# Two row blocks at the end of a stage: block one normed by column halves and turned as two products with the old residual, and the next unit's low part kept over its raw weights

## What is computed

```
def second_block(x, ...):                       # 256 x 1024
    for i in range(2):
        h = rmsnorm(x, mix_pre_gain[i])
        m = fox_mixer(h, ...) if i == 0 else s5_mixer(h, ...)     # each ends in ... @ w_out
        x = x + rmsnorm(m, mix_post_gain[i])                      # pm0, pm1 of the kernel
        h = rmsnorm(x, ffn_pre_gain[i])
        x = x + rmsnorm((silu(h @ w_gate) * (h @ w_up)) @ w_down, ffn_post_gain[i])   # pf0, pf1
    return x

def rmsnorm(x, gain):
    return x * rsqrt(mean(x * x, -1) + 1e-6) * gain
```

## Time and profile before

| | |
|---|---|
| median of three runs | 1037.14 us (1037.1 to 1037.45) |
| the profiled execution, as timed | 1034.07 us |
| its span in the profile | 1032.4 us |
| share of the span in which PE is busy | 96% |
| VectorE, ScalarE, GpSimd busy | 62%, 47%, 31% |
| granted TensorE clock, mean | 0.989 of full |

### The profile page before, as it was taken

How to read it: one execution, slowest core, us unless ns; L and a number is a source line. 1 busy time by engine, 2 the same in 40 slices (tenths; PEclk the granted TensorE clock), 3 DMA queues, 4 the chain that set the end, 5 groups by cost and what they waited for, 6 DMA issues and landing times.

```text
span 1032.4 us, 16878 instructions
## 1 busy us (share of the span) xinstructions
PE 992.5 (96%) x6874; PEld 880.7 (85%) x6874; DVE 635.4 (62%) x653; ACT 482.0 (47%) x632; POOL 324.2 (31%) x316
## 2 busy tenths in 40 slices
PE   8996999999999899999899999999989999999997
PEld 6984779999988778788689999987958989999885
DVE  4899766677654455466675555545676665555534
ACT  5762564444443456545464444434434464444332
POOL 5692047898899211179410000000100010000000
PEclk9997999999999999999999999999999999999999
DMA  9741036777676845544355655556970645555541
GB/s 337 249 163 41 1 123 196 224 221 219 226 236 215 258 125 181 164 138 156 97 182 172 194 172 194 175 192 223 396 298 4 201 142 186 176 190 177 190 163 41
DMA packets 130081, 186.77 MB, mean 181 GB/s; under 512 B 4720, under 2 KB 103536, under 8 KB 129392
## 3 DMA queue, kind: packets, MB, share of 16 engines
q1 hardware_dynamic: 106032, 158.54, 47.0%
q10 hardware_dynamic: 24000, 27.54, 7.9%
HBM read 174.54 MB, written 15.73 MB: 184 GB/s over the span
## 4 chain that ended last, share of the span: by engine, by line
PE 79%; DVE 11%; ACT 4%; issue 3%; DMA 2%; POOL 0%; ACTq 0%; DVEq 0%; POOLq 0%
PE ps L394 13%; PE ps L396 13%; PE ps L395 13%; PE ps L443 7%; PE ps L447 7%; PE ps L445 7%; PE ps L415 3%; PE ps L417 3%; PE ps L416 3%; DVE cacc L1895 3%; DVE wlo L354 2%; ACT whi L348 2%; DMA wraw<-in_s_w_glu 2%; PE ps L821 1%; PE ps L840 1%
## 5 line engine op out<-in xcount | busy, mean ns | idle before, releaser
L354 DVE TENSOR_TENSOR wlo<-wraw,whi 128x2048 fp32r<-128x2048 f32 x143 | 344.6, 2410 | 238.4 <-ACT whi L348 238.4
L348 ACT ACTIVATE whi<-wraw 128x2048 fp32r<-128x2048 f32 x143 | 273.8, 1915 | 378.3 <-PE ps L396 219.6
L394 PE MATMUL ps<-actH,whi 128*128 128x256 f32 x1232 | 351.7, 285 | 1.3 <-DVE actL L565 1.1
L396 PE MATMUL ps<-actH,wlo 128*128 128x256 f32 x1232 | 348.9, 283 | 0.0
L395 PE MATMUL ps<-actL,whi 128*128 128x256 f32 x1232 | 348.8, 283 | 0.0
L394 PEld LDWEIGHTS ps<-actH,whi 128*128 128x128 f32 x1232 | 236.5, 192 | 4.5 <-issue 3.9
L395 PEld LDWEIGHTS ps<-actL,whi 128*128 128x128 f32 x1232 | 236.6, 192 | 0.1
L396 PEld LDWEIGHTS ps<-actH,wlo 128*128 128x128 f32 x1232 | 236.5, 192 | 0.0
L594 POOL TENSOR_SCALAR rs<-ss 128x1 f32<-128x1 f32 (+2 forms) x16 | 4.1, 253 | 603.7 <-ACT nat L580 490.9
L443 PE MATMUL ps<-whi,gH 128*128 128x512 f32 x264 | 82.0, 392 | 0.0
L447 PE MATMUL ps<-whi,gL 128*128 128x512 f32 x264 | 81.4, 390 | 0.0
(11 more groups left out here) (346 smaller groups left out, 1361.4 us busy)
## 6 DMA issues: line engine op xcount, KB each, us to landing
wraw<-in_ffn_w_gate SPq DMA_DIRECT2D x22, 1024.0 KB, 5.3
wraw<-in_ffn_w_up SPq DMA_DIRECT2D x22, 1024.0 KB, 5.3
wraw<-in_ffn_w_down SPq DMA_DIRECT2D x22, 1024.0 KB, 4.9
wraw<-in_fox_w_in SPq DMA_DIRECT2D x16, 1024.0 KB, 5.5
wraw<-in_w_gate SPq DMA_DIRECT2D x11, 1024.0 KB, 5.4
wraw<-in_w_up SPq DMA_DIRECT2D x11, 1024.0 KB, 5.6
wraw<-in_w_down SPq DMA_DIRECT2D x11, 1024.0 KB, 4.9
wraw<-in_w_in SPq DMA_DIRECT2D x9, 1024.0 KB, 11.4
```

Of the source, the lines that this page charges most:

```text
L348: act.activation(self.whi[:, n0 % RING, :], self.wraw[:, n0 % RAW, :], ACT.Copy).then_inc(self.hi_done, 1)
L354: dve.tensor_tensor(self.wlo[:, n0 % RING, :], self.wraw[:, n0 % RAW, :], self.whi[:, n0 % RING, :].bitcast(F32), ALU.subtract).then_inc(s ...
L394: pe.matmul(out, wh, self.actH[:, k, :], start=(i == 0), stop=False)
L396: last = pe.matmul(out, wl, self.actH[:, k, :], start=False, stop=(i == KT - 1))
```

## The change

Nothing of the result's definition changes. The diff's parts:

- **Squares and norms by halves.** At all four seams the accumulator of each row block is squared, and multiplied by the gain, as two halves of 512 columns. ACT and DVE take different halves at a time, and the square goes to `sg` or `prod`. `mm_k_pair` orders block 1 by column half in the last unit and signals `second` when the first half is done. POOL adds the two sums (one more instruction for each block).
- **Block 1 as two products.** PE no longer waits for the new residual of block 1. DVE makes a diagonal matrix of block 1's root, and PE gets each turned tile of block 1 as (old `x_res` tile) times identity plus (`nat` tile) times that diagonal, summed in PSUM, where before there was one transpose. DVE adds block 1 to the residual after its turn (`dve_post_add`). At pf1, where nothing is turned, the addition stays.
- **The first unit of f2, s and f3** (`apart`) is split early: high part to a third buffer `whi3`, low part over its own raw weights. So its raw buffer is free only when PE has used the unit, and the load four places on waits for that (`unit_used`). In the loops over f2 and f3 the same test holds for every second pair, so the gate load of each such pair waits for `unit_used` too.
- **The unit behind it** is split by ACT after its turn and by DVE after its turn and the late addition.
- **The store** of block 1 is in two column halves, the second issued from ACT. The tables `RTab` and `OTab` are loaded once the fourth square of pf0 is done.

```
+        self.wrawlow = at("wrawlow", [P, RAW, UNIT], F32R, self.where["wraw"])
+        self.whi3 = at("whi3", [P, UNIT], F32R, self.where["Uall"])
+        self.apart = (self.first["f2.up"], self.first["s"], self.first["f3.up"])
...
+    def high_of(self, n):
+        return self.whi3[:] if n in self.apart else self.whi[:, n % RING, :]
+
+    def low_of(self, n):
+
+        return self.wrawlow[:, n % RAW, :] if n in self.apart else self.wlo[:, n % RING, :]
+
     def load_unit(self, sp, n0, view, it=0):
 
         n = n0 + 4 * it
         if n0 >= RAW:
-            sp.wait_ge(self.lo_done, n - RAW + 1)
+            sp.wait_ge(self.used if n0 - RAW in self.apart else self.lo_done, n - RAW + 1)
...
-        if n0 >= RING:
+        if n0 >= RING and n0 not in self.apart:
             act.wait_ge(self.used, n - RING + 1)
-        act.activation(self.whi[:, n0 % RING, :], self.wraw[:, n0 % RAW, :], ACT.Copy).then_inc(self.hi_done, 1)
+        act.activation(self.high_of(n0), self.wraw[:, n0 % RAW, :], ACT.Copy).then_inc(self.hi_done, 1)
 
     def split_low(self, dve, n0, it=0):
 
         n = n0 + 4 * it
         dve.wait_ge(self.hi_done, n + 1)
-        dve.tensor_tensor(self.wlo[:, n0 % RING, :], self.wraw[:, n0 % RAW, :],
-                          self.whi[:, n0 % RING, :].bitcast(F32), ALU.subtract).then_inc(self.lo_done, 1)
+        dve.tensor_tensor(self.low_of(n0), self.wraw[:, n0 % RAW, :],
+                          self.high_of(n0).bitcast(F32), ALU.subtract).then_inc(self.lo_done, 1)
...
+        if second is not None:
+            order = order[0:2]
...
+        if second is not None:
+            for c in range(2):
+                out = self.ps[:, base + 2 + c, :]
+                for k in range(2):
+                    h, l = xh[:, k0 + k, P:2 * P], xl[:, k0 + k, P:2 * P]
+                    hi, lo = (t[:, s, k * 1024 + c * 512:k * 1024 + (c + 1) * 512] for t in (self.whi, self.wlo))
+                    pe.matmul(out, h, hi, start=(k0 + k == 0), stop=False)
+                    pe.matmul(out, h, lo, start=False, stop=False)
+                    last = pe.matmul(out, l, hi, start=False, stop=(k0 + k == kn - 1))
+                if c == 0:
+                    last.then_inc(self.sem(second), 1)
...
+            out, cols = self.tp_spot(kt, banks)[:, r * P:(r + 1) * P], slice(kt * P, (kt + 1) * P)
+            if post and r == 1:
+                pe.matmul(out, self.x[:, 1, cols], self.ident[:], start=True, stop=False)
+                last = pe.matmul(out, self.nat[:, 1, cols], self.rdiag[:, 1, :], start=False, stop=True)
+            else:
+                last = pe.transpose(out, self.x[:, r, cols], self.ident[:])
...
+        if post:
+            pe.wait_ge(*self.past(post + "_normed", 4))
+            pe.wait_ge(*self.past(post + "_turn_diag", 1))
+        else:
+            pe.wait_ge(*self.past(ready, 3))
...
+        for i in range(2 * RT):
+            r = i // 2
+            if st[:2] == "pf" and i == 0:
+                act.wait_ge(*self.past(st + "_scale", 1))
+            act.wait_ge(*(self.past(first, 1), self.past(st + "_normed", 1), self.past(first[:2] + "_second", 1),
+                          (self.used, used))[i])
+            if i > 1:
+                act.wait_ge(*self.past(st + "_squares", i - 1))
+            act.activation((self.sg, self.prod)[i % 2][:], self.ps[:, base + i, :], ACT.Square,
+                           scale=self.rx[:, 8 + r:9 + r] if st[:2] == "pf" else D ** -0.5,
+                           accum_out=self.ss[:, i:i + 1]).then_inc(self.sem(st + "_squares"), 1)
...
+    def pool_post_rstd(self, pool, st):
+
+        if st[:2] == "pf":
+            pool.tensor_scalar(self.rx[:, 8:8 + RT], self.rx[:, 0:RT], D ** -0.5, None, ALU.mult)\
+                .then_inc(self.sem(st + "_scale"), 1)
+        for r in range(RT):
+            half, rs = self.ss[:, 8 + r:9 + r], self.rs[:, r:r + 1]
+            pool.wait_ge(*self.past(st + "_squares", 2 * r + 1))
+            pool.tensor_scalar(half, self.ss[:, 2 * r:2 * r + 1], EPS, None, ALU.add)\
+                .then_inc(self.sem(st + "_first_var"), 1)
+            pool.wait_ge(*self.past(st + "_first_var", r + 1))
+            pool.wait_ge(*self.past(st + "_squares", 2 * r + 2))
+            pool.tensor_tensor(rs, self.ss[:, 2 * r + 1:2 * r + 2], half, ALU.add)\
+                .then_inc(self.sem(st + "_var"), 1)
+            pool.wait_ge(*self.past(st + "_var", r + 1))
+            pool.tensor_tensor(rs, rs, self.mhalf[:, 0:1], ALU.pow).then_inc(self.sem(st + "_rstd"), 1)
...
+    def dve_postnorm(self, dve, st, base, gain, gain_ready, gain_value, first):
+
+        def norm(i):
+            h = slice(512 * (i % 2), 512 * (i % 2) + 512)
+            t, acc, g = self.nat[:, i // 2, h], self.ps[:, base + i, :], gain[:, h]
+            if st[:2] == "pf":
+                j = dve.scalar_tensor_tensor(t, acc, self.rx[:, i // 2:i // 2 + 1], g, ALU.mult, ALU.mult)
+            else:
+                j = dve.tensor_tensor(t, acc, g, ALU.mult)
+            j.then_inc(self.sem(st + "_normed"), 1)
 
         dve.wait_ge(*self.past(gain_ready, gain_value))
+        dve.wait_ge(*self.past(first, 1))
+        norm(1)
+        dve.wait_ge(*self.past(st + "_squares", 1))
+        norm(0)
+        dve.wait_ge(*self.past(st + "_squares", 3))
+        norm(2)
+        dve.wait_ge(*self.past(st + "_normed", 2))
+        dve.wait_ge(*self.past(st + "_rstd", 1))
+        self.dve_post_add(dve, st, 0)
+        dve.wait_ge(*self.past(st + "_squares", 4))
+        norm(3)
+        dve.wait_ge(*self.past(st + "_rstd", 2))
+        if st == "pf1":
+            dve.wait_ge(*self.past(st + "_normed", 4))
+            self.dve_post_add(dve, st, 1)
+        else:
+            dve.tensor_scalar(self.rdiag[:, 1, :], self.ident[:], self.rs[:, 1:2], None, ALU.mult)\
+               .then_inc(self.sem(st + "_turn_diag"), 1)
+
+    def dve_post_add(self, dve, st, r):
+
+        for c in range(2):
+            h = slice(512 * c, 512 * c + 512)
+            dve.scalar_tensor_tensor(self.x[:, r, h], self.nat[:, r, h], self.rs[:, r:r + 1], self.x[:, r, h],
+                                     ALU.mult, ALU.add).then_inc(self.sem(st + "_x_ready"), 1)
...
+                for i in range(3):
+                    pair(n + 2 * i, 256 * i, None)
+                with sp.Fori(1, (FP - 1) // 2) as it:
...
-            for r in range(RT):
-                sp.wait_ge(*m.past("pf1_x_ready", 2 * r + 2))
-                sp.dma_start(out[0, r * P:(r + 1) * P, :], m.x[:, r, :]).then_inc(sem("stored"), 16)
-            sp.wait_ge(*m.past("stored", 16 * RT))
+            sp.wait_ge(*m.past("pf1_x_ready", 2))
+            sp.dma_start(out[0, 0:P, :], m.x[:, 0, :]).then_inc(sem("stored"), 16)
+            sp.wait_ge(*m.past("pf1_x_ready", 3))
+            sp.dma_start(out[0, P:2 * P, 0:512], m.x[:, 1, 0:512]).then_inc(sem("stored"), 16)
+            sp.wait_ge(*m.past("stored", 16 * 2))
+            sp.wait_ge(*m.past("last_stored", 16))
...
             m.act_post_squares(act, "pm0", 4, "o2_first", n + 4)
-            m.split_high(act, n + 5)
-            act.wait_ge(*m.past("pm0_normed", RT))
+            act.wait_ge(*m.past("pm0_normed", 2 * RT))
             act.dma_start(m.gb[0][:], io["mix_post_gain_2"][1:2, :].to_broadcast([P, D])).then_inc(sem("gain0_in"), 16)
             m.act_turn(act, "f2", (0, 1, 2, 3, 6, 7), gain=FFNPRE)
+            m.split_high(act, n + 5)
             m.act_pre_squares(act, "f2", "pm0_x_ready")
             m.act_ffn(act, "f2", 4)
 
             n = first["s"]
             m.act_post_squares(act, "pf0", 0, "f2_first", n)
-            m.split_high(act, n + 1)
+            act.wait_ge(*m.past("pf0_squares", 2 * RT))
             act.dma_start(m.RTab[:], m.Rd).then_inc(sem("r_in"), 16)
             act.dma_start(m.OTab[:], m.Od).then_inc(sem("o_in"), 16)
-            act.wait_ge(*m.past("pf0_normed", 2))
+            act.wait_ge(*m.past("pf0_normed", 2 * RT))
             act.dma_start(m.gb[1][:], io["ffn_post_gain_2"][1:2, :].to_broadcast([P, D])).then_inc(sem("gain1_in"), 16)
             m.act_turn(act, "s", (4, 5, 6, 7, 2, 3), gain=MIXPRE + 8)
+            m.split_high(act, n + 1)
             m.act_pre_squares(act, "s", "pf0_x_ready")
...
+            act.wait_ge(*m.past("pf1_x_ready", 4))
+            act.dma_start(Y_OUT[P:2 * P, 512:D], m.x[:, 1, 512:D]).then_inc(sem("last_stored"), 16)
...
-            m.dve_postnorm(dve, "pm0", 4, m.gb[0], "gain0_in", 16)
+            m.dve_postnorm(dve, "pm0", 4, m.gb[0], "gain0_in", 16, "o2_first")
             m.dve_turn(dve, "f2", (0, 1, 2, 3, 6, 7), gain=FFNPRE)
+            m.dve_post_add(dve, "pm0", 1)
             m.split_low(dve, n + 5)
             m.dve_scale(dve, "f2")
             m.dve_ffn(dve, "f2", 4)
             n = first["s"]
-            m.dve_postnorm(dve, "pf0", 0, m.gb[1], "gain1_in", 16)
-
+            m.dve_postnorm(dve, "pf0", 0, m.gb[1], "gain1_in", 16, "f2_first")
```

(1 more changed line is left out.)

77 lines of the change are left out of this document (30 added, 47 removed), and 3 rows, old and new, of the table KINDS.

## The result

The changed kernel takes **1044.96 us** (median of four runs, 1044.42 to 1047.56), the kernel before 1037.12 in the same session (1033.91 to 1037.45). The ratio is 1.0088, 95% interval 1.0062 to 1.0114: slower by 0.9%, +7.8 us, where +5.65 was forecast.

A forecast was written before the change was run, and what follows sets the result against it. PE, busy 96% of the span, was taken to bound the kernel, with its time lost at the seams. Seams 5.25, glu load +1.0 and end -0.6 sum to +5.65 on 1037.14, giving 1042.8 us; range 1037.5 to 1046.5.

The forecast's parts named there:

- Step 1: At the seam, PE begins block 1 at 529.2, 0.5 us earlier than before, since the fills take what DVE saves.
- Step 2: Product pairs at the seam: 26 records take 2.9 us; first product +0.9, late tiles +0.7, together +1.6 us per seam.
- Step 3: Second unit's split by DVE and ACT ties with PE's need: +0.15 us per seam, between 0 and +0.5.
- Step 4: At pf0 the held glu load lands later and delays u's last readout: +1.0 us, ends 0 and +3.2.
- rival of a fair share: The glu load shares bandwidth beside the tables, lands by 740 and costs zero: 1041.8 us; chance 0.10.
- starved load: At pf0 the held glu load costs +3.2 instead of +1.0 us, nothing being freed: 1045.0 us; chance 0.10.
- Step 5: At the end, block 1's earlier addition and the smaller last store give -0.6 us, between -1.2 and +0.3.
- Costed at nothing: POOL's extra instruction, the later second norm and the held gate loads in f2 and f3 were taken to cost nothing.
- Slow pairs: At the seams, records 0.15 us apart make the products cost 4 us more in all: 1046.8 us; chance 0.09.
- cheap pairs: At the seams, a pair costs what one transpose did, so seams come to 0: 1037.5 us, no change; chance 0.15.
- early seam: Early root and diagonal on DVE plus cheap products give 0.7 us per seam, 0.6 at the end: 1034.4 us; chance 0.11.

The follow-up runs named there:

- e1: Changed kernel with the load of OTab moved from ahead of ACT's turn to behind its spread of the roots; 1041.63 us, ratio 1.0047.
- e2: e1 with each tile of block 1 turned by one transpose of the old residual instead of two products; 1035.68 us, ratio 0.9991.
- e6: Changed kernel with the early units' low parts in their ring, so the later loads no longer wait for PE's use; 1041.26 us, ratio 1.0050.
- e7: e6 without the 16 PE fills ahead of block 1; 1040.33 us, ratio 1.0041.
- e8: The changed kernel again, unedited, beside other kernels on one chip; 1043.82 us, ratio 1.0068.
- e3: Changed kernel with 18 more PE fills ahead of its wait for the readout of u; 1043.98 us, ratio 1.0079.
- e4: e1 with block 1 added before the turn and transposed again, second unit split as before, halves and early split kept; 1035.09 us, ratio 0.9997.
- e5: e4 with the early units' low parts in their ring and OTab loaded where the changed kernel loads it; 1033.98 us, ratio 0.9984.

## Where the prediction held and where it failed

**Direction and main term: right.** The pair of products costs more than the halves give, the seams and the glu load slow the kernel, and the end gets shorter. e1 against e2 shows the cause of the first, e6 that of the second. The time, 1044.96, lies inside the range of 1037.5 to 1046.5 and 2.2 us above the forecast of 1042.8.

**Step 1** (PE begins block 1 at 529.2, that is 5.61 after the first square). Measured 5.33. Block 0's addition started 2.71 after the first square (531.27), not 2.86, and the fills' last record ended at 5.50; block 1's first record starts 0.17 ahead of that end, which I had left out. That the fills take all that DVE saves holds only by a hair: e7 gives 0.07 us for them, and right behind stands the diagonal.

**Step 2** (26 records in 2.95, +1.6 a seam). The 26 records took 2.87 (533.89 to 536.76), 0.110 each, so the price from the earlier trace rows held, and its lower value was the right choice. The reason that I gave for it, a PE warmed by fills, is not what the trace of before shows: the granted clock was 1.00 from 7 to 11 too, where the records lay 0.15 apart, and what spread them there is not shown. By the four passes of the Trainium skill (FP8 and Floating Point Precision, TensorE Precision Notes) I had estimated 0.213 us a product; these took 0.22. First product +0.56 instead of +0.92, late tiles 6 records or +0.67, as said. What stands in the trace for step 2 is +1.23.

**Step 3** (a tie, +0.15). It is 0.3, the wait of 0.19 and 0.1 behind it. DVE's split ended 15.05 after the first square, forecast were 15.31; PE wanted it at 14.92. With it a seam costs 1.58 in f and 1.67 at pf0 instead of 1.75: 4.83 in all, forecast 5.25.

**Step 4** (+1.0): **the step that failed**, by its size. The cost is 2.23, still within the ends of 0 and 3.2 that I gave. The hold itself came when it was said (issue 15.35 after the first square; 15.5 forecast). Two sizes were off. I had OTab's landing 26.4 after the first square, since a unit's 1 MB leaves its stretch; it came at 27.05, as OTab took 23.2 us and not 22.7. And the glu unit landed 4.4 behind OTab, not 4.0. Together they make 1.0 of the difference of 1.23. The other 0.2 is the rounding down from 1.2 for the second glu split, for which there was no row. The rival of a fair share fell: the load took 16.07 us for 1 MB in the changed kernel, 16.06 in e8 and 16.35 in e3, and landed behind all of the table. The Trainium skill (DMA: Bandwidth & Descriptors, Queues, rings and completion order) has the engines take turns between queues packet by packet. Equal shares of the bytes did not come of it here; no run tells whether the turns or their sizes differ. The starved load (+3.2) was nearer than my own value.

**What no step had: the clock behind the wait.** I took every stretch at full clock. In both traces of the changed kernel the clock fell with PE's wait ahead of the transposes, of 3.41 and 3.40 us. It was worth 2.5 us in the first (3.67 + 2.78 against 1.97 + 1.94) and 1.6 in e8; e3, in which PE has fills there, and e6, in which it waits 1.17, show none. For the profiled execution this and step 4 are more than the miss: 5.65 was forecast and the stretches give 8.43, with +1.23 from step 4 and +2.13 behind u, less 0.42 at the seams and 0.17 at the end. By the medians the held load and the fallen clock cost 2.56 together (e8 against e6), not the 4.8 of the traces, and I can't say how often the clock falls there, since only one execution of a kernel has a trace.

**Step 5** (-0.6). The end is 0.77 shorter, 0.70 in e8. Block 1's addition comes 5.11 after the first square instead of 5.28, and the last store takes 2.1 instead of the 2.6 of the earlier trace rows:

```profile
out<-x_res SPq DMA_DIRECT2D x1, 512.0 KB, 2.7
out<-x_res SPq DMA_DIRECT2D x1, 256.0 KB, 2.1
out<-x_res ACTq DMA_DIRECT2D x1, 256.0 KB, 2.1
```

**Costed at nothing.** The held gate loads cost nothing, as said (f of e6 against f of the changed kernel). POOL's extra instruction has no run of its own.

**The rivals.** Slow pairs and cheap pairs fell by the 0.110 us a record and the 26 records. The early seam had two faults. Its sign, 2.5 us of norm and addition of block 1 in the earlier trace rows, was misread, since from 527.75 to 529.72 these rows have 1.97. And its sum leaves out the +1.0 of step 4, which pairs don't touch. The part of it that was right is in e4 and e5: with transposes behind the halves a seam does get 0.3 to 0.45 shorter.

**What stays open.** In e1, e6 and e7 no glu load holds up the readout, and they are 5.1, 5.8 and 4.9 us above before by the medians, 4.9, 5.2 and 4.2 by the ratios. Their stretches account for 4.1 (4.83 less 0.7). The rest is near the width of the intervals. The traces of e1 and e7 show clock falls in the scan (0.73 and 0.67 in the window from 775), but with one trace of each kernel I can't tell whether the changed kernel has more of them than the kernel before.
